# Values stationary in the second block's attention, mLSTM heads in pairs, and buffers kept at 128-byte places

## The reference, cut to what matters

```
# first block, mLSTM: per head of 64 query/key and 128 value columns
dmat = bcum[..., :, None] - bcum[..., None, :] + igc[..., None, :]      # -inf above the diagonal
p = jnp.exp(dmat - m_t[..., None]) * jnp.einsum('bhcld,bhcsd->bhcls', qc, kc)
num = sc_inter * (qc @ c_prev) + jnp.einsum('bhcls,bhcsv->bhclv', p, vc)
h = num / jnp.maximum(jnp.abs(den), jnp.exp(-m_t))                      # then rmsnorm per head, times sigmoid(mo)
# second block, attention: 8 heads of 64 columns (4 plain, 4 with a forget term in the logits)
p = jax.nn.softmax(logits, axis=-1)
out = jnp.einsum('bhqk,bhkd->bhqd', p, v)                               # heads side by side, then @ w_o
# second block, pooling: sums over windows of 2, 4, 8, 16 tokens, from a cumulative sum, minus the input, times w_g
```

## Time and profile before

| what | value |
|---|---|
| median of 3 runs | 1938.76 us |
| time of the profiled execution | 1938.86 us |
| its span, first to last instruction | 1936.8 us |
| TensorE (PE) busy | 1923.4 us, 99% |
| PE weight loads (PEld) busy | 1661.8 us, 86% |
| VectorE (DVE) busy | 1303.1 us, 67% |
| ScalarE (ACT) busy | 1124.1 us, 58% |
| granted TensorE clock, mean | 0.999 |
| HBM traffic | 172 GB/s over the span |
| chain that ended last | PE 92%, DVE 6%, ACT 1%, DMA 1% |

### The profile page before, as it was taken

How to read it: one execution, slowest core, us unless ns; L and a number is a source line. 1 busy time by engine, 2 the same in 40 slices (tenths; PEclk the granted TensorE clock), 3 DMA queues, 4 the chain that set the end, 5 groups by cost and what they waited for, 6 DMA issues and landing times.

```text
span 1936.8 us, 28378 instructions
## 1 busy us (share of the span) xinstructions
PE 1923.4 (99%) x10940; PEld 1661.8 (86%) x10940; DVE 1303.1 (67%) x2242; ACT 1124.1 (58%) x1797; POOL 6.5 (0%) x18
## 2 busy tenths in 40 slices
PE   9999999999999999999999999999999999999998
PEld 7888899899888888888989998888988888988887
DVE  5555787566655575558875666555858888858886
ACT  5444766554644564456774656445747666647665
POOL 0000000000000000000000000000000000000000
PEclk9999999999999999999999999999999999999999
DMA  8655545536555556655455456665535565535563
GB/s 280 187 186 184 172 132 168 169 126 201 193 186 188 180 181 189 186 162 174 138 168 165 152 164 215 186 192 153 167 114 188 184 187 180 168 115 187 184 188 96
DMA packets 93685, 335.75 MB, mean 173 GB/s; under 512 B 10224, under 2 KB 12528, under 8 KB 93552
## 3 DMA queue, kind: packets, MB, share of 16 engines
q1 hardware_dynamic: 92112, 328.51, 53.5%
q0 software_dynamic: 720, 4.37, 0.6%
q10 hardware_dynamic: 720, 1.07, 0.2%
HBM read 332.86 MB, written 1.05 MB: 172 GB/s over the span
## 4 chain that ended last, share of the span: by engine, by line
PE 92%; DVE 6%; ACT 1%; DMA 1%; issue 0%; SPq 0%; DVEq 0%; ACTq 0%
PE stream L1841 10%; PE stream L1843 9%; PE stream L1842 9%; PE acc L1841 9%; PE acc L1843 9%; PE acc L1842 9%; PE stream L2322 7%; PE stream L1835 7%; PE stream L1836 6%; PE stream L1837 6%; PE stream L2323 3%; DVE w_lo L1075 1%; PE stream L1935 1%; PE acc L2248 1%; PE acc L2045 1%; DVE conv_tiles L1540 1%
## 5 line engine op out<-in xcount | busy, mean ns | idle before, releaser
L1075 DVE TENSOR_TENSOR w_lo<-w_raw,w_hi 128x1024 fp32r<-128x1024 f32 x624 | 759.5, 1223 | 365.1 <-ACT w_hi L558 363.4
L558 ACT ACTIVATE w_hi<-w_raw 128x1024 fp32r<-128x1024 f32 x624 | 654.5, 1054 | 374.5 <-PE stream L1843 207.1
L1841 PE MATMUL stream<-w_hi,h_both 128*128 128x512 f32 x896 | 354.0, 395 | 0.0
L1843 PE MATMUL stream<-w_lo,h_both 128*128 128x512 f32 x896 | 349.2, 390 | 0.0
L1842 PE MATMUL stream<-w_hi,h_both 128*128 128x512 f32 x896 | 348.8, 389 | 0.0
L1835 PE MATMUL stream<-h_both,w_hi 128*128 128x256 f32 x800 | 234.4, 293 | 0.0
L1836 PE MATMUL stream<-h_both,w_hi 128*128 128x256 f32 x800 | 226.0, 282 | 0.0
L1837 PE MATMUL stream<-h_both,w_lo 128*128 128x256 f32 x800 | 225.9, 282 | 0.0
L2322 PE MATMUL stream<-h_both,w_hi 128*128 128x512 f32 x608 | 217.4, 400 | 0.0
L1841 PE MATMUL acc<-w_hi,act_hi 128*128 128x512 f32 x528 | 211.1, 400 | 1.6 <-DVE conv_sums L1532 1.3
L1843 PE MATMUL acc<-w_lo,act_hi 128*128 128x512 f32 x528 | 206.3, 391 | 0.0
(11 more groups left out here) (332 smaller groups left out, 2613.4 us busy)
## 6 DMA issues: line engine op xcount, KB each, us to landing
w_raw<-in_w_up SPq DMA_DIRECT2D x264, 512.0 KB, 3.5
w_raw<-in_w_mix SPq DMA_DIRECT2D x228, 512.0 KB, 3.5
w_raw<-in_w_down SPq DMA_DIRECT2D x132, 512.0 KB, 3.5
params<-in_params POOLq DMA_DIRECT2D x4, 859.5 KB, 6.7
out_x<-x_residual SPq DMA_DIRECT2D x4, 256.0 KB, 2.7
constants<-in_consts POOLq DMA_DIRECT2D x1, 832.0 KB, 7.4
x_residual<-in_x ACTq DMA_DIRECT2D x3, 256.0 KB, 6.7
x_residual<-in_x SPq DMA_DIRECT2D x1, 256.0 KB, 3.8
```

Source lines behind the costliest of these rows:

```text
L558: nc.scalar.activation(w_hi[:, u % RING], w_raw[:, u % RAW], ACT.Copy).then_inc(hi_ready, 1)
L1075: nc.vector.tensor_tensor(w_lo[:, u % RING], w_raw[:, u % RAW], w_hi[:, u % RING].bitcast(F32), ALU.subtract).then_inc(split_done, 1)
L1841: nc.tensor.matmul(dst, hi, w_hi[:, s, w], start=first, stop=False)
L1843: return nc.tensor.matmul(dst, hi, w_lo[:, s, w], start=False, stop=last)
```

## The change

Five edits:

- **Values stationary.** In step 19 v (128 x 64 of one head) is stationary and `aT8` moves (256 and 128 columns). Two heads write the two halves of the output's partitions. The result is already turned, so `o_scale` and `turn_o` go. The division by the row sums moves ahead of the transposes: `inverse(h)` on VectorE in step 9 + h (for the last head in step 15, ahead of the last window sums) and `attn_share(h)` on ScalarE, two instructions per head, in the same step; `turn_a(h)` waits for it. `o_round` and `o_rest` move to step 20.
- **Heads in pairs.** `mlstm_scores(p)` runs for two heads, in steps 48, 52, 56 and 60; the values follow in 49, 50, 53, 54, 57, 58, 61 and 62. The decay's first 256 columns lie in halves of `bank[3]`, its last 128 behind the keys in `side[0]` or `side[1]`. The keys of the two heads use the two halves of the array's rows. The row selection for the 256 columns uses all 128 rows (`sel_low`, zero in the lower half).
- **Turns moved.** `ym_turn`, `ym_round` and `ym_rest` are in steps 63, 64, 66 and 68; the copy of heads 6 and 7 is in step 62, their statistics and root in step 63.
- **One wait moved.** Of the first w_down unit the products into `acc_tok[0]` no longer wait for the tiles of i = 3.
- **Buffers.** `sel_low` and a pad of 64 bytes each are added, `decay` has two buffers, `o_tok` goes. The buffers behind `row_select` move by 128 bytes or by multiples of it.

```diff
+        sel_low, _ = sb("low_select", [P, HEADS], F32R)
+        sb("low_select_pad", [P, 16])
-        zw, _ = sb("decay", [P, 3 * P])
+        zw, _ = sb("decay", [P, 2, 3 * P])
-        o_tok, _ = sb("o_tok", [P, QT, 2 * T])
-        YM_TURN = (57, 63, 65, 68)
+        YM_TURN = (63, 64, 66, 68)
+        PAIR_AT = (48, 52, 56, 60)
+        NUM_AT = tuple(PAIR_AT[h // 2] + 1 + h % 2 for h in range(HEADS))
+        def early_decay(h):
+            return bank[3][:, h % 2 * T:h % 2 * T + T]
+        def late_decay(h):
+            return side[h % 2][:, 3 * P:]
+        def keys(h):
+            return side[h % 2][:, 0:3 * P]
-        HEAD_AT, TURN_AT, VALUES_AT, OUT_TURN_AT = 8, 10, 19, 21
+        HEAD_AT, TURN_AT, VALUES_AT, OUT_AT = 8, 10, 19, 20
...
                 def mlstm_exp(h):
                     act.wait_ge(mlstm_sc, n8 + h + 1)
-                    if h > 0:
-                        act.wait_ge(mp_ready, n8 + h)
+                    act.wait_ge(mlstm_qk, n8 + h + 1)
+                    if h > 1:
+                        act.wait_ge(mp_ready, n8 + h - 1)
...
-                    if i >= U_GL and i % 2 == 0 and i < U_GL + 16:
-                        mlstm_exp((i - U_GL) // 2)
+                    if i in PAIR_AT:
+                        mlstm_exp(2 * PAIR_AT.index(i))
+                        mlstm_exp(2 * PAIR_AT.index(i) + 1)
                     for g, (a, z) in enumerate(GROUPS):
-                        if i == U_GL + 1 + 2 * (z - 1):
+                        if i == NUM_AT[z - 1]:
                             take_num(g)
-                        if i == U_GL + 2 + 2 * (z - 1):
+                        if i == NUM_AT[z - 1] + 1:
                             mlstm_rstd(g)
                     if i in YM_TURN:
                         ym_round(YM_TURN.index(i))
...
+                def attn_share(h):
+                    act.wait_ge(e2_inverse, l * 8 + h + 1)
+                    b = h % 2
+                    nc.scalar.activation(sm[:, b, 0:P], sm[:, b, 0:P], ACT.Copy, scale=rden[:, h, 0:1])
+                    nc.scalar.activation(sm[:, b, P:3 * P], sm[:, b, P:3 * P], ACT.Copy,
+                                         scale=rden[:, h, 1:2]).then_inc(e2_share, 1)
...
+                def inverse(h):
+                    dve.wait_ge(e2_ready, l * 8 + h + 1)
+                    nc.vector.reciprocal(rden[:, h], den[:, h]).then_inc(e2_inverse, 1)
...
                     if i == 15:
                         c_rest()
+                        inverse(HEADS - 1)
                     if i == 14:
                         window_sums(0)
                     if i == 15:
                         window_sums(1)
...
+                    heads = (2 * p, 2 * p + 1)
+                    for h in heads:
+                        nc.tensor.matmul(early_decay(h), ident_r[:], neg_r[:, 0:T], start=True, stop=False)
+                        nc.tensor.matmul(late_decay(h), ident_r[:], neg_r[:, T:3 * P], start=True, stop=False)
+                        nc.tensor.matmul(early_decay(h), sel_low[:, h:h + 1].to_broadcast([P, P]), nm[:], start=False,
+                                         stop=True)
+                    for h in heads:
+                        r = slice(64 * (h % 2), 64 * (h % 2) + 64)
+                        nc.tensor.matmul(late_decay(h), sel_r[r, h:h + 1].to_broadcast([64, P]), nm[r, P:T], start=False,
+                                         stop=True).then_inc(mlstm_sc, 1)
+                    for c, ks, qs in ((slice(0, T), slice(0, P), slice(0, T)), (slice(T, 3 * P), slice(P, T), slice(P, T))):
+                        for h in heads:
+                            r = slice(64 * (h % 2), 64 * (h % 2) + 64)
+                            i = nc.tensor.matmul(keys(h)[:, c], y[r, 4 + h // 2, ks], y[r, h // 2, qs], start=True,
+                                                 stop=True)
+                            if c.start > 0:
+                                i.then_inc(mlstm_qk, 1)
...
                 def ym_turn(p):
                     pe.wait_ge(ym_ready, n8 + 2 * p + 2)
                     if p == 0:
-                        pe.wait_ge(ya_split, l * 4 + 4)
+                        pe.wait_ge(mp_ready, n8 + HEADS)
                     else:
                         pe.wait_ge(ym_split, n8 + 2 * p)
...
                         hi, lo = operand(u)
                         for t in range(QT):
+                            if d == 0 and t == 1:
+                                pe.wait_ge(conv_in, 2 * (l * (NF - 2) + 1) + 2)
                             r = wide_rows(u, hi, lo, t, d == 0, False)
...
                 def turn_a(h):
-                    pe.wait_ge(e2_ready, l * 8 + h + 1)
+                    pe.wait_ge(e2_share, l * 8 + h + 1)
...
+                    for g in range(2):
+                        for k in range(2):
+                            for a, c in enumerate((slice(k * T, k * T + T), slice(k * T + P, k * T + T))):
+                                for j in range(2):
+                                    h = 4 * g + 2 * k + j
+                                    r = nc.tensor.matmul(bank[2 - 2 * g][64 * j:64 * j + 64, c],
+                                                         v_tok[:, a, 64 * h:64 * h + 64],
+                                                         aT8[:, h, 0:T] if a == 0 else aT8[:, h, T:3 * P],
+                                                         start=(a == 0), stop=(a == 1))
+                        r.then_inc(o2_ready, 1)
-                def turn_o():
-                    for t in range(QT):
-                        pe.wait_ge(o2_scaled, l * 2 + t + 1)
-                        for k in range(4):
-                            r = nc.tensor.transpose(bank[2 * t + 1][:, blk(k)], o_tok[:, t, blk(k)], ident)
-                        r.then_inc(o2_turned, 1)
```

More of the change, by code:

```diff
@@ L425, in build @@
         e2_ready = sem("e2_ready")
+        e2_inverse = sem("e2_inverse")
+        e2_share = sem("e2_share")
         a2_turned = sem("a2_turned")
@@ L970, in d_round, with o_round @@
                     r.then_inc(cd_hi, 1)
[L972 to L974 removed]
+                def o_round(g):
+                    act.wait_ge(o2_ready, l * 2 + g + 1)
+                    nc.scalar.activation(ya_hi[:, 2 * g:2 * g + 2], bank[2 - 2 * g][:].rearrange("p (k t) -> p k t", k=2),
                                          ACT.Copy).then_inc(o2_hi, 1)
@@ L997, in mixer2 @@
                 for i in range(1, U_MIX2 - LAG + 1):
-                    if i == OUT_TURN_AT:
-                        o_round(0)
-                        o_round(1)
+                    if i == HEAD_AT + HEADS:
+                        attn_share(HEADS - 1)
                     hi_next()
@@ L1003, in mixer2 @@
                         attn_store(i - TURN_AT)
+                    if HEAD_AT < i < HEAD_AT + HEADS:
+                        attn_share(i - HEAD_AT - 1)
                     if HEAD_AT <= i < HEAD_AT + HEADS:
@@ L1022, in mixer2 @@
                         take_values(1)
+                    if i == OUT_AT:
+                        o_round(0)
+                        o_round(1)
                 layer_norm(l, 0, "ln1_g", "ln1_b")
@@ L1338, in mlstm_p @@
                         dve.wait_ge(num_ready, n8 + h - 1)
-                    nc.vector.scalar_tensor_tensor(out=mp[:, h % 2], in0=side[0][:, 0:3 * P], scalar=A_SCALE,
-                                                   in1=zw[:], op0=ALU.mult, op1=ALU.mult).then_inc(mp_ready, 1)
+                    nc.vector.scalar_tensor_tensor(out=mp[:, h % 2], in0=keys(h), scalar=A_SCALE,
+                                                   in1=zw[:, h % 2], op0=ALU.mult, op1=ALU.mult).then_inc(mp_ready, 1)
                 def mlstm_stats(g):
@@ L1443, in mixer @@
                         conv(i - 1 - U_MQK)
-                    if U_GL <= i < U_GL + 16 and i % 2 == 0:
-                        mlstm_p((i - U_GL) // 2)
+                    if i in PAIR_AT:
+                        mlstm_p(2 * PAIR_AT.index(i))
+                        mlstm_p(2 * PAIR_AT.index(i) + 1)
                     for g, (a, z) in enumerate(GROUPS):
-                        if i == U_GL + 2 + 2 * (z - 1):
+                        if i == NUM_AT[z - 1] + 1:
                             mlstm_stats(g)
-                        if i == U_GL + 3 + 2 * (z - 1):
+                        if i == NUM_AT[z - 1] + 2:
                             mlstm_out(g)
@@ L1721, in mixer2 @@
                 for i in range(U_MIX2 - LAG + 1):
+                    if HEAD_AT < i < HEAD_AT + HEADS:
+                        inverse(i - HEAD_AT - 1)
                     if HEAD_AT <= i < HEAD_AT + HEADS:
@@ L2087, in mlstm_scores @@
                         pe.wait_ge(sc_masked, (n8 + HEADS) * 2)
+                        pe.wait_ge(ya_split, l * 4 + 4)
                     else:
-                        pe.wait_ge(mp_ready, n8 + h)
-                    r = slice(64 * (h % 2), 64 * (h % 2) + 64)
```

(13 more changed lines are left out.)

59 lines of the change are left out of this document (18 added, 41 removed).

## The result

| kernel | median, us | range, runs | ratio to before |
|---|---|---|---|
| before | 1939.19 | 1938.73 to 1939.84, 11 | |
| after | 1943.78 | 1941.45 to 1944.93, 11 | 1.0024 [1.0015, 1.0032] |

The change made the kernel slower by 4.6 us, and the ranges of the two kernels don't overlap; forecast was 1933.8 us with a range of 1930.0 to 1937.8. By the forecast's own borders the result is a slower kernel, to which it gave 0.06. The profiled execution of the kernel after took 1941.45 us (span 1939.6), the fastest of its eleven: 2.6 us above that of before.

A forecast was written before the change was run, and what follows sets the result against it. TensorE's own instruction list was taken as the bound. Against 1938.86 us, -5.3 - 5.9 - 1.3 + 6.1 + 0.2 + 1.2 = -5.0 gave 1933.8 us, with an 8-in-10 range of 1930.0 to 1937.8.

The forecast's parts named there:

- the last sentence of its sum of parts: Buffers behind the pad: places kept modulo 128 bytes, so moved addresses cost 0, bounded by +-0.5 us.
- the clock's rival: Behind the first-block mixers' stalls the clock falls to half: +1.5 us per stall, +3 in all, 1936.8 us; chance 0.15.
- Pairs: mLSTM scores: two heads together take 1.78 us instead of 2.44; four pairs in two layers, -5.3 us.
- Values: Second mixer: stationary values on overlapping column halves take 3.3 us per layer instead of 6.27; two layers, -5.9 us.
- The row of one round: First block's attention: 0.85 us for one round with its end, backing 0.75 per values round instead of 0.64.
- conv_sums: Convolution's start: six matmuls go first and cover TensorE's two waits of 0.65 us, -1.3 us.
- ym_turn(1): Step 64 of first-block mixers: TensorE idles 3.0 us per layer for `ym_rest(0)` behind statistics and root, +6.1 us.
- values(6): Step 61: waits for both products of step 60, +0.2 us in both layers together.
- second mixer's added work: Shares and inverses on ScalarE and VectorE delay the rotation 0.15 and the pooling 0.45 us per layer; together +1.2 us.
- The columns do overlap: Rejects the rival that column halves don't overlap for accumulating pairs: values save only 1.7, time 1938.0 us; chance 0.07.
- ScalarE is not the bound in steps 10 to 16: Rejects the rival that second-mixer `turn_a(h)` waits for `attn_share(h)`: some 3.5 us lost per layer, 1940.8 us; chance 0.07.
- that of the hidden stall: First-block mixers: TensorE's stall ahead of the moved turn doesn't appear, no +6.1, time 1927.7 us; chance 0.08.

The follow-up runs named there:

- b_128: Kernel before with one unused buffer of 128 bytes behind `row_select`, nothing else; 1945.96 us, ratio 1.0034.
- after_again: The kernel after, unchanged, run once more for a second profile; 1943.38 us, ratio to before 1.0021.
- a_256: Kernel after with its pad at 192 bytes, so buffers behind it keep their old place modulo 256 bytes; 1934.90 us, ratio to before 0.9979.
- a_order: Kernel after with `ym_round` moved ahead of copy and root on ScalarE, `ym_rest` ahead of the statistics on VectorE; 1934.21 us, ratio to before 0.9974.
- b_act128: Kernel before with 128 unused bytes ahead of `act_hi`, places of weights and `h` kept; 1943.13 us, ratio 1.0023.
- best: Kernel after with both the 192-byte pad and the reordered `ym_round` and `ym_rest` calls; 1926.98 us, ratio to before 0.9939.
- b_64: Kernel before with 64 unused bytes behind `row_select`; 1942.87 us, ratio 1.0018.

## Why the prediction was wrong

**The step that failed** is the last sentence of its sum of parts: "The pad keeps every old buffer at the same place modulo 128 bytes, so the moved addresses are costed at 0; the trace before shows no row on it, and I bound it by +-0.5." It cost 6.9 us as `b_128` measures it. Two things were wrong. The pad was sized for a period of 128 bytes that no row shows (the runs have 128 off slow and 256 off free), and a bound was given to something for which there was no row. What stood in reach was the exposure: the `act` groups alone have 1584 matmuls, so that each ns more per matmul is 1.6 us, and half a microsecond bounds them to 0.3 ns; they became 4 to 5 ns slower. With the term the sum would have been +1.9 us, a kernel of 1940.7. What is left to the measured 1943.8 is what the clock's rival would have added (3 us); that the two fill the gap so exactly is in part luck, since the smaller terms below miss by up to 0.7 each way.

**The clock.** A fall behind the stall was a rival at 0.15, with 1.5 us per stall, for which there was no row. It happened, at 1.4, 1.5 and once 2.7 us, and in some executions only. "Full load stands on both sides" was no protection. In the three profiles of kernels with the stall it costs 1.4, 4.2 and 0 us, and it goes with the spread between executions: the kernels that keep the stall range over 3.5 us (after), 4.9 (after_again) and 5.4 (a_256), those without it over 1.1 (before) and 1.5 (a_order). The mean granted clock of the runs says the same: 0.998 in the fastest runs of after and after_again (1941.45 and 1940.14 us) and 0.996 in their slowest (1944.93 and 1945.04), never below 0.998 on record for before and a_order. Not all spread is of this kind: `b_act128`, without the stall, ranges over 3.8 us at 0.998 to 0.999.

**Right, with sizes:**
- Pairs: 1.78 us forecast; 1.75 and 0.11 of exit measured, -4.6 us for -5.3. The 128-column matmul cost less than taken (0.06 for 0.09), but the change to half rows more: 360.58 - 360.32 = 0.26 us behind a matmul of 0.12, 0.14 and not 0.10.
- Values: 3.3 us forecast, 2.96 measured; -6.6 us for -5.9. A round took (2.75 - 0.1) / 4 = 0.66 us against 0.75: overlap is better than strict order of issue says and close to the full 0.64. The row of one round misled, since it held the end too.
- `conv_sums`: -1.8 us for -1.3, 0.9 per layer where the wait itself was 0.65. Where the other quarter is from stays open.
- `ym_turn(1)`: 3.0 us forecast, 2.93 and 2.92 measured. The chain read from step 64 shows the same links, the root's wait of 2.75 us even in its second decimal. But it was treated as given. It was the largest term against the change, and reordering two calls takes it away.
- `values(6)`: +0.1 us for +0.2; second mixer's added work +0.6 for +1.2: the pooling comes 0.3 us later in each layer and not 0.45, and the wait for the rotation stayed at 0.5 (it was 1.1 in `best`, see above).
- The columns do overlap, and ScalarE is not the bound in steps 10 to 16: TensorE has no wait on its scores ahead of the turns. These two rivals are out, as is that of the hidden stall. They held all of the 0.06 given to a slower kernel, so this direction was not foreseen for the reason that it came.

## What to carry over

A buffer added or removed in front of others can be an edit of every matmul whose operands lie on its two sides: move places by 256 bytes, the one distance that was free in these runs, or take the price from a run with an unused buffer of the same size, which separates it from the change in one comparison. When a large change moves the time little, compare first the groups that the change doesn't touch; their mean of one (390 to 395 ns) gave away more than any wait. And a wait in an in-order list is to be asked what stands behind it: here 5.9 us of stall and the clock's fall came from a root that the rounding behind it did not need.

## What the runs showed of the chip

- Matmuls of 512 moving fp32r columns with a stationary tile of activations stand 227 or 232 ns apart by the distance of the two operands' places: 0 and 256 bytes from the old distance 227, 64 and 128 bytes 232. Moving `act` and `ya` against the weights costs the kernel 6.9 us of 1939, moving `h_both` too 17.7.
- The opposite case, `w_hi` stationary and 512 columns of `h_both` moving, went from 237.9 to between 233.0 and 236.3 ns in the same runs, also in those that moved neither of its operands (`b_128`, `b_act128`, `b_64`). The cause of neither is known.
- Behind a stall of 2.9 us amid full load the granted clock was down at 0.5, its level of 1.2 GHz, in three of six cases, at a cost of 1.4, 1.5 and 2.7 us.
